# Recurrent units of a hybrid RG-LRU / SGU / conv-FFN layer: the decay's square at the unit's end on VectorE, joins and weight splits moved around it

## The reference

```python
h = _modulated_norm(x, norm_mix_g[l], shift1, scale1)
z = h @ w_in[l]                       # 1024 x 1024 @ 1024 x 6144
xr, gr, zu, zv, ga, gb = jnp.split(z, split_idx, axis=-1)
xr = _causal_dwconv(xr, rnn_conv_w[l], rnn_conv_b[l])      # 4 taps
y_a = _rg_lru(xr, lru_w_a[l], lru_b_a[l], lru_w_x[l], lru_b_x[l], lru_lambda[l])
y_a = (y_a * jax.nn.gelu(gr)) @ w_branch_a[l]
...
def _rg_lru(x, w_a, b_a, w_x, b_x, lam):
    r = jax.nn.sigmoid(_block_diag(x, w_a, b_a))           # 8 blocks of 128 x 128
    i = jax.nn.sigmoid(_block_diag(x, w_x, b_x))
    log_a = LRU_C * r * jax.nn.log_sigmoid(lam)
    a = jnp.exp(log_a)
    mult = jnp.sqrt(-jnp.expm1(2.0 * log_a))
    u = mult * (i * x)
    _, h = lax.associative_scan(_lin_combine, (a, u), axis=1)
    return h
```

## Time and profile before

| | before |
|---|---|
| median of 3 runs | 1542.42 us (1542.19 to 1542.64) |
| profiled execution, its own time | 1542.83 us |
| its span | 1540.8 us |
| PE busy | 1516.1 us (98%), clock at full speed all through |
| DVE busy | 1222.6 us (79%) |
| ACT busy | 811.0 us (53%) |
| POOL busy | 381.7 us (25%) |

### The profile page before, as it was taken

The page is one execution under the profiler, slowest core; times in us unless marked ns, Lnnn a source line. Parts: engine busy times, 40 slices in busy tenths (PEclk is TensorE's granted clock), DMA queues, the critical chain, the costliest instruction groups (busy, mean ns, idle before and its releaser), DMA issues.

```text
span 1540.8 us, 19510 instructions
## 1 busy us (share of the span) xinstructions
PE 1516.1 (98%) x6820; PEld 1241.4 (81%) x6820; DVE 1222.6 (79%) x1484; ACT 811.0 (53%) x1207; POOL 381.7 (25%) x291
## 2 busy tenths in 40 slices
PE   7999999999999999999999999999999999999998
PEld 4778777788888888888887788888888888888887
DVE  6987988745656685478868999999999987778786
ACT  5368888645555461012534555555555553444447
POOL 0023434422222200000010333333333331233224
PEclk9999999999999999999999999999999999999999
DMA  9532222312332347574421144444444446677722
GB/s 347 180 105 60 89 69 79 96 55 82 106 103 66 110 150 233 181 246 146 164 62 35 48 150 161 154 150 150 151 151 151 150 130 229 229 242 252 238 89 110
DMA packets 199984, 219.56 MB, mean 142 GB/s; under 512 B 8944, under 2 KB 155728, under 8 KB 199120
## 3 DMA queue, kind: packets, MB, share of 16 engines
q1 hardware_dynamic: 199888, 218.32, 42.8%
HBM read 160.61 MB, written 57.67 MB: 142 GB/s over the span
## 4 chain that ended last, share of the span: by engine, by line
PE 76%; DVE 15%; ACT 4%; issue 3%; DMA 1%; POOL 0%; SPq 0%; ACTq 0%; DVEq 0%; POOLq 0%
PE ps L807 57%; PE ps L880 10%; DVE wop L1834 4%; DVE hidw L2466 1%; PE ps L1158 1%; PE ps L1067 1%; PE ps L1010 1%; PE ps L1140 1%; DVE ps L1848 1%; PE ps L965 1%; DVE part_acc L1897 1%; ACT wop L1221 1%; DVE yq L1932 1%; DVE tn L1927 1%; DVE ti L2039 1%
## 5 line engine op out<-in xcount | busy, mean ns | idle before, releaser
L1221 ACT ACTIVATE wop<-raw 128x512 fp32r<-128x512 f32 (+1 forms) x529 | 299.8, 570 | 419.2 <-PE ps L807 162.0
L1834 DVE TENSOR_TENSOR wop<-raw,wop 128x512 fp32r<-128x512 f32 (+1 forms) x529 | 385.5, 736 | 165.1 <-ACT wop L1221 161.8
L807 PE MATMUL ps<-yq,wop 128*128 128x512 f32 x1680 | 405.2, 390 | 1.3 <-DVE wop L1834 0.7
L807 PEld LDWEIGHTS ps<-yq,wop 128*128 128x128 f32 x1680 | 314.3, 188 | 71.2 <-issue 3.9
L649 POOL TENSOR_TENSOR raw<-raw,raw 128x512 f32<-128x512 f32 (+1 forms) x65 | 96.4, 1483 | 863.3 <-DVE wop L1834 377.5
L807 PE MATMUL ps<-dq,wop 128*128 128x512 f32 x840 | 191.3, 389 | 0.5 <-DVE wop L1834 0.5
L807 PEld LDWEIGHTS ps<-dq,wop 128*128 128x128 f32 x840 | 157.4, 188 | 34.2 <-issue 1.2
L807 PE MATMUL ps<-t4q,wop 128*128 128x512 f32 x528 | 128.5, 392 | 2.0 <-DVE ps L1848 1.9
L807 PE MATMUL ps<-t2q,wop 128*128 128x512 f32 x528 | 127.7, 391 | 1.8 <-DVE wop L1834 1.0
L807 PE MATMUL ps<-t3q,wop 128*128 128x512 f32 x528 | 127.9, 391 | 0.8 <-ACT snap_u L1236 0.8
L807 PE MATMUL ps<-t1q,wop 128*128 128x512 f32 x528 | 127.7, 391 | 0.0
(11 more groups left out here) (266 smaller groups left out, 1978.9 us busy)
## 6 DMA issues: line engine op xcount, KB each, us to landing
dq<-hid_keep SPq DMA_DIRECT2D x35, 1024.0 KB, 7.3
raw<-in_w_in SPq DMA_DIRECT2D x96, 256.0 KB, 3.3
raw<-in_w_up SPq DMA_DIRECT2D x96, 256.0 KB, 3.3
hid_keep<-part_b SPq DMA_DIRECT2D x40, 512.0 KB, 3.0
ada_ring<-in_w_ada SPq DMA_DIRECT2D x32, 512.0 KB, 4.6
hid_keep<-part_t SPq DMA_DIRECT2D x20, 512.0 KB, 2.8
raw<-in_w_down SPq DMA_DIRECT2D x80, 128.0 KB, 2.4
ada_w<-in_w_ada SPq DMA_DIRECT2D x8, 1024.0 KB, 11.5
```

The lines of the kernel that those rows point to most:

```text
L807: done = nc.tensor.matmul(bank, left[:, w, lk, :], right[:, x, rk, :], start=(first and w == 0 and x == 0), stop=(last and w == 1), skip_g ...
L1221: nc.scalar.activation(wop[n % 4][:, 0, 0:depth[n], :], raw[slot][:, 0:depth[n], :], ACT.Copy).then_inc(f_hi, 1)
L1834: V.tensor_tensor(wop[n % 4][:, 1, 0:kd, :], raw[slot_of[n][0]][:, 0:kd, :], wop[n % 4][:, 0, 0:kd, :].bitcast(F32), ALU.subtract).then_in ...
```

## The change

Five edits, all of order; no instruction is added or taken away.

- `decay_square(m)` on VectorE moves from step 1 of the second unit after R m to step 6 of the first, between the low parts of the next unit's second and third weights.
- The second join comes before the low part of n0 + 7 instead of behind it, and the third before that of n0 + 8.
- The low part of n0 + 3 stands between the second and the third convolution tap, with the tap's wait on its forerunner kept.
- In ScalarE's `decay` the high part of n0 + 8 comes behind exp and square instead of between tanh and exp.
- In ZV 1 ScalarE's first snap comes before the second gelu of ZV 0's tiles.

```diff
--- before.py
+++ after.py
@@ -1393,7 +1393,6 @@
                     act.wait_ge(m2_ready, m)
                 nc.scalar.activation(th[:, :], la_a[:, :], ACT.Tanh, bias=la4n[:, m:m + 1],
                                      scale=la4n[:, m:m + 1]).then_inc(ach, 1)
-                weights(n)
                 act.wait_ge(ach, 2 * m + 1)
                 nc.scalar.activation(la_a[:, :], la_a[:, :], ACT.Exp, bias=la4[:, m:m + 1],
                                      scale=la4[:, m:m + 1]).then_inc(ach, 1)
@@ -1401,6 +1400,7 @@
                 if m:
                     act.wait_ge(tail_step, m)
                 nc.scalar.activation(m2[:, :], la_a[:, :], ACT.Square).then_inc(th_ready, 1)
+                weights(n)
 
             def decay_root(m):
                 act.wait_ge(m2_ready, m + 1)
@@ -1469,11 +1469,13 @@
                 m, m_past = prev_unit(pos, "R"), prev_unit(pos, "R", 2)
                 b = V_BLOCK[pos] if pos in V_BLOCK else None
                 for w in range(7):
-                    if w in (1, 2, 3):
+                    if w in (1, 2, 3) and (w > 1 or SEQ[pos] != ("ZV", 1)):
                         snap(pos, w - 1)
                     if m is not None and w == 2:
                         conv_high(m)
                     if w == 0:
+                        if SEQ[pos] == ("ZV", 1):
+                            snap(pos, 0)
                         if m is not None:
                             block_diag_high(m)
                         elif pos > 2:
@@ -2004,14 +2006,19 @@
             lo(10)
 
 
-            def conv(m, banks):
+            def conv(m, banks, weights, n):
                 x, src = xc[m % 2], flat(banks[0])
                 dve.wait_ge(tap0, m + 1)
                 for d in range(1, CW):
+                    if d == CW - 1:
+                        weights(n)
+                        dve.wait_ge(vch, middle)
                     tap = V.scalar_tensor_tensor(x[:, d:S], src[:, 0:S - d], C("rnn_conv_w", (CW - 1 - d) * KT + m), x[:, d:S],
                                                  ALU.mult, ALU.add)
-                    if d < CW - 1:
+                    if d < CW - 2:
                         step(tap)
+                    elif d == CW - 2:
+                        middle = step_number(tap)
                 tap.then_inc(conv_done, 1)
 
             def block_diag_low(m):
@@ -2090,18 +2097,21 @@
                 b = V_BLOCK[pos] if pos in V_BLOCK else None
                 past = BANKS[(pos - 1) % 2]
                 for w in range(7):
-                    if w >= 4:
+                    if w == 4 or w >= 4 and m is None:
                         join(pos, w - 4)
-                    if m is not None and w == 5:
-                        gated_input(m)
                     if m is not None:
+                        if w == 4:
+                            join(pos, 1)
+                        if w == 5:
+                            gated_input(m)
+                            join(pos, 2)
+                        if w == 6:
+                            decay_square(m)
                         if w == 0:
-                            conv(m, past)
+                            conv(m, past, lo, n0 + 3)
                             block_diag_low(m)
                         if w == 1:
                             conv_low(m)
-                    if m_past is not None and w == 1:
-                        decay_square(m_past)
                     if m_past is not None and w == 3:
                         scan_input(m_past)
                         scan(m_past)
@@ -2127,7 +2137,8 @@
                     if item == ("ZU", 3):
                         for k in ((), (), (), (0, 1), (2, 3), (), (4, 5))[w]:
                             ya_low(k)
-                    lo(n0 + w + 3)
+                    if w or m is None:
+                        lo(n0 + w + 3)
 
 
             def ada_piece(e, k):
```

## The result

The changed kernel takes 1545.94 us (median of 12 runs, 1544.84 to 1547.38) against 1542.64 us of the kernel before (12 runs): a ratio of 1.0021 with a 95% interval of 1.0014 to 1.0029. It is 3.3 us slower; 3.5 us and 1545.9 were predicted.

A forecast was written before the change was run, and what follows sets the result against it. A ring of VectorE and GpSimd turns, 22.48 us a round, was taken as the bound, not TensorE's waits. R 2 +0.17, five rounds +3.45 and ZV 0's scan -0.09 gave +3.5 us, median 1545.9; range 1538.8 to 1547.4.

The forecast's parts named there:

- A ring of VectorE and GpSimd turns: Convolution to convolution in the recurrent units: work repeating every 22.48 us sets the pace; 23.16 us after the change.
- Low part between the taps: Low part of n0 + 3: product 3's wait goes, but the last tap ends at 4.40 instead of 3.90 us.
- Square out of step 1: Second unit, ahead of the scan: ScalarE's root starts 0.61 us sooner against the taps' end; VectorE idles there instead.
- Joins, exp and square ahead of the high part, ZV 1's snap: Joins and later high part cost nothing; the snap can remove 0.82 us at product 2, but product 6 stays late.
- Square in step 6: Behind L656: square and L660 are held, so the next convolution starts 11.19 us behind the scan's end, 0.78 later.
- rival hand-over: In step 6: VectorE keeps the turn behind square, 1539.1 us, nearly all of 0.23; square beats L656, convolution 0.92 later.
- Where TensorE waits: Per unit: old waits go and reappear as 1.4 us at products 2, 3 and the block-diagonal product.
- The sum: Whole kernel: 0.17 + 3.45 - 0.09 = +3.5 us, median 1545.9 us, 0.23% slower.
- R 2's round: Round from R 2's convolution: root's 0.61 us won and 0.78 lost, +0.17 at the next convolution.
- The five rounds: Full rounds up to ZV 0's convolution: each 0.69 us longer, 3.45 in all.
- The walk for ZV 1: Product 6 waits for the second join, hence the scan, and starts +3.5 us late whatever was won ahead.
- all waits vanish: Recurrent stage: if all TensorE waits went, 4.8 us would go, giving 1537.6 us.

The follow-up runs named there:

- third-buffer kernel: Kernel before with GpSimd's gate multiplication in two halves, the second after the four weight sums, and a third gelu gate buffer: 1536.36 us, ratio 0.9958.
- the half multiplication: Kernel before with GpSimd's gate multiplication in two halves, the second after the four weight sums, beside the taps: 1539.01 us, ratio 0.9977.

## Why the prediction held, point by point

- **The bound.** A ring of VectorE and GpSimd turns, not TensorE's waits: shown. The ring was forecast at 23.16 and measured at 23.14 us; with the ring at 22.32, 22.22 and 21.77 the time went to 1540.2, 1539.0 and 1536.4, whatever TensorE's waits were named after.
- **Low part between the taps.** +0.50 us at the end of the taps was forecast, exposed because VectorE would wait for ScalarE in its old place; it does, for 0.80 us. The last tap now starts 3.10 us behind the first (224.23 - 221.13) and ends 4.37 behind its start, where it was 3.90 before: +0.47. The undoing of it alone took 2.7 us off. Right.
- **Square out of step 1.** 0.6 us sooner for the root against the taps' end and idle time in VectorE were forecast. The root starts 2.93 us behind the taps' end instead of 3.53, and 0.47 us of idle time stand ahead of `scan_input`. Right.
- **Joins, exp and square ahead of the high part, ZV 1's snap.** Costed at nothing: a ratio of 1.0000 with them alone. Right there. In the changed kernel, where the square's move also brings R 2's scan forward, the join's wait shifts the turns in that unit, as shown above; neither the joins alone nor the square alone does it.
- **Square in step 6.** 2.3, 2.1 and 1.8 us forecast for square, L660 and low part; 2.31, 2.06 and 1.77 measured. Right. Neither rival hand-over occurred: VectorE never kept the turn behind the square, and the square never beat a waiting L656. The one short square, in R 2's unit, comes after L656 is done.
- **Where TensorE waits.** Products 2 and 3 wait and product 6 does not, as forecast. The wait forecast at the block-diagonal product is not in the rows: `conv_low` ends at 227.86, and the product could not have started before 227.92, a pitch behind product 3.
- **The sum.** +3.5 forecast; the matmuls stand 3.46 us later behind ZV 1 and the medians 3.3. Two terms were off and cancelled, by luck. R 2's round was to give +0.17 and gave +0.34 (151.69 against 151.35), since the walk missed the join that waits for product 4 there (11.35 us behind the scan's end, not 11.19). The five rounds were to give 5 x 0.69 = 3.45 and gave 3.28 (267.41 - 151.69 against 263.79 - 151.35), 0.66 each. Forecast and measured alike, ZV 0's convolution is 3.62 us late. That the median came out within 0.1 us of 1545.9 is luck too: the kernel before was at 1542.64 here and not at 1542.42. The walk for ZV 1 (product 6 late whatever the snap gains) held: +3.46 there.
- **One number was wrong and carried nothing.** The most that TensorE could win in the stage was put at 4.8 us, by nine units of 21.76. ZV 1 has no block-diagonal product, so it is 200.66 - 8 x 21.76 - 7 x 2.72 = 7.5 us, with the small transposes in it, and the third-buffer kernel took 6.5 of them. The bound of 1537.6 for "all waits vanish" was thus too high, and the expectation for it was made with the count mended.

What is not settled: why the first waiting operation gets the turn nearly always but not always. In the kernel before, L649 starts 0.158 to 0.161 us behind a VectorE operation at 881.52, 918.63 and 955.52 and loses the next turn; L656 starts 0.162 us behind one at 864.69, with VectorE's next operation just as ready, and gets it.

## What to carry to other kernels

The engine with 98% busy time (TensorE) was not what set the pace of this stage: its waits were where a ring of the other engines, VectorE's and GpSimd's turns above all, touched it. Before an instruction is moved to where the busy engine waits, follow one full round of the work from a point back to itself, count what is held by whom, and ask whether the wait that is to be removed is a link of it. Two-input SBUF work of GpSimd is best placed beside VectorE's PSUM work: the half multiplication that cost a turn behind the scan ran unhindered beside the taps (1.30 us). It became free only with a third buffer for what it holds.

## What the runs showed of the hardware

- VectorE and GpSimd operations with two SBUF inputs exclude each other for their whole length, in turns. A waiting 512-column fp32 sum on GpSimd ended 1.14 to 1.15 us after VectorE's operation, a waiting 512-column one on VectorE 0.54 to 0.56 us after GpSimd's. A GpSimd operation of 128 columns took 1.23 us while VectorE's 1024-column square ran, and 0.46 us without it.
- The turn mostly goes to the operation that has waited longer, though VectorE's next is ready without a gap: in all six rounds of L660 in the changed kernel and in all six of L652 before. Over the whole kernel before, GpSimd got it 19 times of 22. Three operations of L649 in the channel sub-layer lost it, as in the earlier trace rows.
- VectorE operations with one input in PSUM were not held: the join took 0.69 us beside GpSimd's whole multiplication, and the three taps 3.90 us beside its second half.
